# A fused transformer pair on one core: how many context slabs run alone before the middle of the expert gather

## The reference

```
u_sel = peer_u[expert]
a = gelu(einsum('bqhkd,bqd->bqhk', u_sel, hb))
v_sel = peer_v[expert]
return einsum('bqhk,bqhkd->bqd', g * a, v_sel)
```

```
x   = x   + 0.5*g1x*swiglu(modulate(rmsnorm(x,   norm_ffn1), sh1x, sc1x), w13_ffn1, w2_ffn1)
ctx = ctx + 0.5*g1c*swiglu(modulate(rmsnorm(ctx, norm_ffn1), sh1c, sc1c), w13_ffn1, w2_ffn1)
```

## Time and profile before

| | us |
|---|---|
| median of 3 runs (lowest, highest) | 1755.93 (1754.56, 1759.41) |
| the profiled execution, own time | 1749.51 |
| its span, first to last instruction | 1747.7 |
| PE busy, PEld busy | 1643.7, 1490.3 |
| DVE busy, ACT busy, POOL busy | 1124.2, 644.4, 411.7 |

### The profile page before, as it was taken

The page is one execution under the profiler, slowest core; times in us unless marked ns, Lnnn a source line. Parts: engine busy times, 40 slices in busy tenths (PEclk is TensorE's granted clock), DMA queues, the critical chain, the costliest instruction groups (busy, mean ns, idle before and its releaser), DMA issues.

```text
span 1747.7 us, 29476 instructions
## 1 busy us (share of the span) xinstructions
PE 1643.7 (94%) x11948; PEld 1490.3 (85%) x11948; DVE 1124.2 (64%) x1933; ACT 644.4 (37%) x1230; POOL 411.7 (24%) x327
## 2 busy tenths in 40 slices
PE   5999889996899899999999989999999999999997
PEld 3977779996898789998898558989999986989997
DVE  3675548985997497688888661227466447656554
ACT  4434323332332353333112134515444532444443
POOL 0553424442444444344443310000000000000000
PEclk8999999997999999999999999999999999999999
DMA  9668699999999999999999999785345530455442
GB/s 385 242 270 361 246 424 419 403 400 422 406 409 420 420 371 421 422 421 421 416 413 422 422 372 414 294 339 208 107 187 193 193 145 7 187 192 194 178 166 91
DMA packets 58307, 542.71 MB, mean 311 GB/s; under 512 B 6464, under 2 KB 6592, under 8 KB 7744
## 3 DMA queue, kind: packets, MB, share of 16 engines
q1 hardware_dynamic: 21168, 271.37, 39.3%
q0 software_dynamic: 37008, 269.50, 37.6%
HBM read 539.80 MB, written 1.05 MB: 309 GB/s over the span
## 4 chain that ended last, share of the span: by engine, by line
PE 57%; DMA 20%; DVE 12%; issue 7%; ACT 2%; POOL 1%; SPq 0%; POOLq 0%; DVEq 0%; ACTq 0%
PE psum L486 57%; DMA arena<-in_experts,idx_stage 17%; DVE arena L2296 4%; DMA ring<-in_w_ada 2%; DVE arena L2285 1%; DMA ring<-in_w_ffn 1%; POOL arena L1252 1%; DMA ring<-in_w_in 1%; DVE arena_r L1865 0%; DVE ring_r L1799 0%; DVE small L2285 0%; DVE x_t L2199 0%; DVE arena L2407 0%; DVE rstd L1856 0%; DVE arena L1956 0%
## 5 line engine op out<-in xcount | busy, mean ns | idle before, releaser
L2285 DVE CUSTOM_DVE_ANT_0 arena<-arena 128x1024 f32<-128x1024 f32 x256 | 313.7, 1225 | 147.2 <-DMA arena<-in_experts,idx_stage 141.1
L1252 POOL DMA_INDIRECT arena<-in_experts,idx_stage x256 | 303.3, 1185 | 363.7 <-DVE arena L2296 157.6
L486 PE MATMUL psum<-h_t,ring 128*128 128x128 f32 (+1 forms) x2064 | 327.7, 318 | 4.9 <-ACT h_t L1544 2.1
L1799 DVE TENSOR_TENSOR ring_r<-ring,ring_r 128x1024 fp32r<-128x1024 f32 (+1 forms) x172 | 207.1, 1212 | 185.3 <-ACT ring_r L1305 184.4
L486 PEld LDWEIGHTS psum<-h_t,ring 128*128 128x128 f32 x2064 | 298.1, 191 | 31.0 <-issue 7.6
L486 PE MATMUL psum<-small_r,ring_r 128*128 128x256 f32 x1600 | 285.5, 282 | 4.1 <-DVE h_t_r L1886 4.1
L486 PE MATMUL psum<-small,arena 128*128 128x128 f32 x2080 | 252.5, 283 | 33.7 <-ACT small L1662 33.7
L486 PEld LDWEIGHTS psum<-small,arena 128*128 128x128 f32 x2080 | 247.9, 199 | 37.6 <-ACT small L1662 32.1
L486 PEld LDWEIGHTS psum<-small_r,ring_r 128*128 128x128 f32 x1600 | 244.7, 188 | 6.1 <-issue 5.8
L1305 ACT ACTIVATE ring_r<-ring 128x1024 fp32r<-128x1024 f32 (+1 forms) x172 | 178.8, 1046 | 164.0 <-PE psum L486 148.4
L486 PE MATMUL psum<-arena_r,ring_r 128*128 128x256 f32 x1552 | 229.6, 283 | 1.3 <-DVE arena_r L1865 1.3
(11 more groups left out here) (264 smaller groups left out, 1570.6 us busy)
## 6 DMA issues: line engine op xcount, KB each, us to landing
ring<-in_w_ffn SPq DMA_DIRECT2D x35, 2048.0 KB, 11.2
ring<-in_w_in SPq DMA_DIRECT2D x31, 2048.0 KB, 8.7
ring<-in_w_ada SPq DMA_DIRECT2D x25, 2048.0 KB, 10.5
ring<-in_w_ffn SPq DMA_DIRECT2D x24, 1408.0 KB, 7.5
arena<-in_w_ada SPq DMA_DIRECT2D x5, 2048.0 KB, 13.8
ring<-in_w_out SPq DMA_DIRECT2D x4, 2048.0 KB, 8.7
ring<-in_peer_wq SPq DMA_DIRECT2D x4, 2048.0 KB, 12.7
ring<-in_p_ret SPq DMA_DIRECT2D x4, 2048.0 KB, 7.4
```

The costliest lines, as they stand in the source:

```text
L486: return nc.tensor.matmul(o, a, b, start=first, stop=last)
L1252: nc.gpsimd.indirect_dma_start(rows[slot % GBUF], None, dram["experts"], bass.IndirectOffsetOnAxis(ap=idx_stage[:, slot:slot + 1], axis=0) ...
L1799: nc.vector.tensor_tensor(whole(i, ring_r), whole(i, ring), upper(i).bitcast(F32), ALU.subtract).then_inc(lo_made, 1)
L2285: step(nc.vector.tensor_tensor_reduce(u, u, h2[:, n // PER_TILE, :], 1.0, 0.0, ALU.mult, ALU.add, dots[:, n % 8, s:s + 1]), sem("dots"))
```

## The change

`ALONE` goes from 2 to 3 and `HELD` from 2 to 1:

```
-ALONE, HELD = 2, 2
+ALONE, HELD = 3, 1
```

## The result

The changed kernel takes 1776.05 us (median of 4 runs, 1775.09 to 1777.61) beside 1757.26 us for the kernel before (4 runs): the ratio is 1.0121, 95% interval 1.0102 to 1.0141. It is slower, by 18.8 us between the medians and 21 by the ratio. Forecast were 13.0 us more, 1768.9; the range ended at 1776.0. Measured again beside other kernels, the ratio was 1.0116 (1.0094 to 1.0137). Each cost is uncertain by 2 to 4 us, so that a difference of two costs is uncertain by 3 to 6 us, and the plain difference of the medians can lie up to 2.5 us away from it.

The account below looks back on a forecast made before the run. The gather was taken as bound by a full DMA path, with TensorE nearly full too. Slab bytes 5.0, TensorE 1.0, crossing 6.3 and clock 0.7 gave 13.0 us over 1755.9: 1768.9 us, own range 1764 to 1774, wider 1758 to 1776.

Parts of the forecast that it names:

- Which stage is full, and the price of a slab: In the gather, rows and slabs share a full DMA path; a sixth first-half slab load costs +5.0 us, low end 0.
- TensorE in the first half, +1.0 us: Four more context chunks, 13.98 us of work, mostly fit TensorE's 29 us of waits: +1.0 us, ends 0 and 6.
- the sum of 6.0: First half of the gather: 5.0 us for the slab's bytes and 1.0 us for TensorE's four more chunks.
- The crossing: Between the gather's halves, holding one slab makes TensorE and VectorE wait: +6.3 us, ends 0 and 14, plus clock 0.7.
- TensorE's pause: In the crossing, after the squares TensorE has nothing to do until h_first: 15.5 us instead of 1.7.
- VectorE's waits: Behind the crossing, VectorE's turns come too early and it waits for TensorE in batches 68 to 74: 14.0 us.
- 6.3 + 0.7: Crossing: 14.0 us of new waits less 7.0 of row waits and 0.7 of a context multiply; 0.7 for the clock.
- The clock fell in the pause as said: After TensorE's pause in the crossing the granted clock drops for a while: +0.7 us, between 0 and 3.5.
- The sum: Whole kernel: 5.0 + 1.0 + 6.3 + 0.7 = 13.0 us more, giving 1768.9 us.
- (a): Only the slab's bytes count in the gather; buffers hide VectorE's waits, DMA ends 5 to 6 us later: 1761, chance 0.20.
- (b): Not slower: the sixth slab fills DMA holes in the first half, TensorE sets the gather's end: 1755, chance 0.10.
- (c): Worse: schedule stays tight past batch 77 through three rereads, clock drops in each pause: 23.5 us, 1779, chance 0.12.

Follow-up runs that it names:

- start30: The changed kernel with the first context chunk planned one batch later (CTX_START = 30), ScalarE's square staying at batch 31: 1.0078, 13.7 us over the kernel before.
- the later turns: VectorE's and ScalarE's turns for token halves of slabs 3 to 5 and context halves of 4, 5 two batches later; on the changed kernel 1.0082, 14.4 us.
- alone3_held2_start30: The kernel before with ALONE = 3, HELD still 2 and CTX_START = 30: extra slab and chunks in the first half; 1.0035, 6.1 us over before.
- bytes_only: The kernel before with slab 0 loaded twice for the context in the first half, no other work moved: 1.0029, 5.1 us over before.
- alone3_held2: The kernel before with ALONE = 3, HELD still 2: the extra slab and its four chunks in the first half; 1.0078, 13.7 us over before.
- chunks_early: The kernel before with slab 2's four context chunks in the first half, no extra load, CTX_START = 30, squares of x before slab 3: 1.0027, 4.7 us.

## Why the prediction was wrong

- **Which stage is full, and the price of a slab**: right, within 2.1 to 7.9 us. 5.0 forecast, 5.1 measured alone by the ratio, 3.6 between the medians and at the end of tile 0; the even 2.49 us between rows told it.
- **TensorE in the first half, +1.0 us, ends 0 and 6: the step that failed.** The step looked at TensorE's slack (29 us for 14) and not at where the plan puts the first of its chunks and what that one waits for: handed over at batch 30 and not 31, the sum of the context's squares held TensorE 8.95 us and not 3.99. Of the 14.2 us there, 8 or so were not in the sum of 6.0. About 7 are the longer pause (traces); timed it is worth 6.6 (changed less start30), 7.6 (with HELD = 2) and 4.4 (with the later turns). The four chunks themselves took up to 3.5, and not 1.0. My upper end of 6, meant for four chunks without slack, did not hold a wait at all.
- **The crossing**: right in place and kind, and in size within what the runs can tell. TensorE's pause 15.49 for 15.5; VectorE's waits 13.0 for 14.0; timed, start30 less alone3_held2_start30 is 7.6 for 6.3 + 0.7. The second half is 8.5 us longer, but 3.5 of them are there without this pause too (below), which leaves 5 in the traces. The clock fell in the pause as said: 0.69 of full speed at 650 to 660 us, and the token half of slab 3 took 8.75 us for the 7.3 of before, 1.4 more where 0.7 were summed. That the turns of VectorE and ScalarE cost more than TensorE's pause is shown by the traces: behind tile 0 the gather ends 8.5 to 9.6 us later with both (four traces), 4.1 to 5.2 with the pause and later turns (three), 3.5 and 3.6 with neither. The timed pairs agree but less sharply: 4 to 6 us for the turns, 1 to 4 for the pause.
- **The sum**: 5 + 1 + 7 = 13 was forecast. The steps from the kernel before to the changed one are 6.1 for slab and chunks (alone3_held2_start30), 7.6 for the crossing and 6.6 for the longer pause, 20.3; as differences along one path they must add up to the measured cost, so this proves nothing by itself. The term that the forecast lacks altogether is the 6.6. That the range ended only 0.05 us short of the result is chance; the 6 to 8 us missing from the sum are not.
- **Rivals**: (a) and (b) fall, by bytes_only and the waits; in (b), rows did not land at the old times. (c) had the size nearly right for a reason that did not show: VectorE caught up after batch 74 as said, and the three rereads brought no lasting lag (22 to 23.5 us at slots 180 to 224, 22.7 at the end).
- **What stays open**: 3 to 4 us behind the middle that ALONE = 3 costs even with HELD = 2 (from 617.36 to 1041.47, 424.1 us, against 420.7; 3.6 in the trace of alone3_held2). VectorE never waits for TensorE there, but TensorE once for VectorE's L2224, 7.7 and 8.3 us in the two traces, which the kernel before does not have. Whether that is the loss was not tried. The third reread is not needed for such a loss: chunks_early, which has none, loses 4.2 us there, with its own pause of 11.6 us. In the timed 6.1 us of alone3_held2_start30 little room is left for it. Open, too, is how much of start30's gain comes from the three chunks that moved with the sum of squares.

## What to carry to other kernels

When a constant changes how much work a written plan spreads over steps, list for every unit the step before and after, the first unit above all, and for each the step in which its input is made: rounding moves units by one step, and a unit that arrives one step before its data holds everything queued behind it. Slack of the engine was no cover for that here, since what was lost was not the engine's time but the requests that the queue behind it would have made to the full resource. And ask of a pause which queue stands behind it: 15.5 us of TensorE with no row behind them cost 1 to 4 us, a pause of 9 us and not 4 with rows behind it cost 3 to 8, and 11 us fewer waits on VectorE gave back 4 to 6.

## What the runs showed of the hardware

Executions of one kernel on one chip differ by up to 0.7% here (1747.74 to 1759.32 in 23 runs of the kernel before), and the traces show one source of such differences: behind the gather, where all versions have the same code, the granted clock falls in some traces and not in others, after the same short pauses of TensorE. In the changed kernel it stands 1.88 and 1.70 us about 1200 us and the clock granted at 1202 to 1212 us is 0.52, near the lower level; in the kernel before it stands 1.64 and 1.72 us at the same place and the clock at 1180 to 1190 us is 1.00; in start30 it stands 1.91 and 1.72 us and the clock at 1194 to 1204 us is 1.00. A single trace's span is thus no measure of a change of 0.3%; stage ends counted from a common point within it are better, and even they move: counted from its own first row, tile 0 ends 14.1 us late in one trace of the changed kernel and 16.1 in the other.
